# One VectorE instruction for both one-hot matrices of four tokens, with the weights multiplied in on ScalarE

## What is computed

```
q = (x @ w_q).reshape(T, PEER_HEADS, 2, PEER_DQH)
scores = einsum('thsd,hskd->thsk', q, sub_keys)        # 128 keys in each of two halves
s, i = top_k(scores, 16)
cand = s[:, :, 0, :, None] + s[:, :, 1, None, :]       # 16 x 16 pairs
top, sel = top_k(cand, 16)
idx = i0 * 128 + i1 of the selected pairs              # 8 heads x 16 experts a token
g = softmax(top)
a = gelu(einsum('td,thkd->thk', x, u_tab[idx]))
out = einsum('thk,thkd->td', g * a, v_tab[idx])
```

## Time and profile before

| | |
|---|---|
| median of 3 runs | 4314.09 us (4311.28 to 4319.12) |
| the profiled execution | 4313.75 us, span 4311.9 us |
| mean granted TensorE clock | 0.965 |
| busy: TensorE, VectorE, ScalarE, GpSimd | 94%, 61%, 11%, 33% of the span |
| layer 0, first scatter to last | 1228.9 to 1619.2 us |
| layer 1, first scatter to last | 3264.5 to 3622.3 us |

### The profile page before, as it was taken

One profiled execution on the slowest core, in us unless ns is written; L12 is line 12 of the kernel. 1 busy time (PEld: TensorE's weight loads), 2 busy tenths in 40 slices (PEclk: granted clock), 3 DMA queues, 4 the chain that ended last, 5 costly groups with the idle time before them and its releaser, 6 DMA issues.

```text
span 4311.9 us, 35262 instructions
## 1 busy us (share of the span) xinstructions
PE 4059.6 (94%) x12920; PEld 2247.2 (52%) x12920; DVE 2616.0 (61%) x5488; ACT 473.0 (11%) x879; POOL 1440.1 (33%) x1072
## 2 busy tenths in 40 slices
PE   8997899989999998999998999999999986999998
PEld 1655555555555663444444545666656664444443
DVE  2303577767767884433434954888887887443444
ACT  2010111101111220000001121111112221000000
POOL 0000014444445553333320000454555565333331
PEclk9998999999999998999999999999999986999999
DMA  8111247778889999888873100788889999888875
GB/s 318 60 58 62 93 171 288 282 269 314 313 314 348 355 343 374 318 331 322 316 281 123 59 30 20 280 313 298 328 330 342 353 330 321 356 328 321 321 304 184
DMA packets 349757, 1128.44 MB, mean 262 GB/s; under 512 B 23424, under 2 KB 139632, under 8 KB 328712
## 3 DMA queue, kind: packets, MB, share of 16 engines
q0 software_dynamic: 153632, 560.15, 35.2%
q1 hardware_dynamic: 96880, 515.69, 31.0%
q10 hardware_dynamic: 99072, 50.33, 3.9%
HBM read 1025.01 MB, written 101.07 MB: 261 GB/s over the span
## 4 chain that ended last, share of the span: by engine, by line
PE 88%; DMA 6%; DVE 5%; ACT 1%; issue 0%; SPq 0%; ACTq 0%; POOL 0%; DVEq 0%
PE bank L652 88%; DMA ring<-in_peer_ut 2%; DMA peer_gates<-work 2%; DMA ring<-in_peer_w_q 1%; DVE bc L1366 1%; DVE diag L1354 1%; DVE ring L1336 1%; DVE bc L1368 1%; DMA ring<-in_ada_w 1%; ACT work L952 0%; ACT hT L952 0%; DMA bc<-peer_gates 0%; DVE work L1190 0%; DVE work L1192 0%; PE bank L696 0%
## 5 line engine op out<-in xcount | busy, mean ns | idle before, releaser
L652 PE MATMUL bank<-hT,ring 128*128 128x384 f32 (+3 forms) x5696 | 1808.5, 477 | 59.5 <-DMA ring<-in_peer_ut 30.3
L652 PEld LDWEIGHTS bank<-hT,ring 128*128 128x128 f32 x5696 | 1062.0, 193 | 728.0 <-issue 89.2
L612 POOL DMA_INDIRECT ring<-in_peer_u,work x512 | 769.9, 1504 | 1728.4 <-DVE ring L1336 1456.6
L652 PE MATMUL bank<-ring,work 128*128 128x512 f32 x2016 | 868.8, 592 | 0.0
L612 POOL DMA_INDIRECT ring<-in_peer_v,work x512 | 644.5, 1259 | 302.1 <-issue 155.6
L1354 DVE SCALAR_TENSOR_TENSOR diag<-ring,work,diag 128x1024 f32<-128x1024 f32 x508 | 652.8, 1285 | 29.5 <-DMA ring<-in_peer_v,work 26.1
L1336 DVE SCALAR_TENSOR_TENSOR ring<-ring,work 128x1024 f32<-128x1024 f32 x512 | 622.2, 1215 | 22.7 <-DMA ring<-in_peer_u,work 22.7
L652 PEld LDWEIGHTS bank<-ring,work 128*128 128x128 f32 x2016 | 383.0, 190 | 482.2 <-issue 482.2
L1393 DVE TENSOR_TENSOR work<-work,bc 128x1536 f32<-128x1536 f32 x64 | 112.4, 1758 | 717.2 <-PE bank L652 666.0
L952 ACT ACTIVATE work<-bank 128x384 f32<-128x384 f32 (+3 forms) x540 | 290.7, 541 | 2029.8 <-PE bank L652 1928.6
L652 PE MATMUL bank<-work 128*128 128x512 f32 x1056 | 461.3, 597 | 30.8 <-DVE work L1393 30.8
(11 more groups left out here) (156 smaller groups left out, 1595.1 us busy)
## 6 DMA issues: line engine op xcount, KB each, us to landing
ring<-in_peer_ut SPq DMA_DIRECT2D x64, 2048.0 KB
ring<-in_peer_vt SPq DMA_DIRECT2D x42, 2048.0 KB, 7.9
ring<-in_ada_w SPq DMA_DIRECT2D x24, 2048.0 KB, 14.4
peer_gates<-work ACTq DMA_DIRECT2D x48, 1024.0 KB
bc<-peer_gates SPq DMA_DIRECT2D x32, 1536.0 KB
peer_acts<-work SPq DMA_DIRECT2D x60, 768.0 KB
work<-peer_acts SPq DMA_DIRECT2D x60, 768.0 KB, 15.1
work<-in_peer_vt SPq DMA_DIRECT2D x22, 2048.0 KB, 7.9
```

The lines of the kernel that those rows point to most:

```text
L612: nc.gpsimd.indirect_dma_start(row, None, table, bass.IndirectOffsetOnAxis(ap=idx_all[:, i:i + 1], axis=0)).then_inc(s, 16)
L652: return nc.tensor.matmul(out, lhsT, rhs, start=start, stop=stop, **kw)
```

## The change

`hot` no longer multiplies by the weights. One tensor_tensor compares both index rows of four tokens with the row 0..127 and writes all eight matrices. A new step `scale` on ScalarE then multiplies the first matrix of each of the four tokens by its weights, in place, and raises `oh_scaled`, for which `scatter` now waits. The planner's cost of a hot encoding falls from 2.1 to 1.3, and the times at which it deems the next steps due move. The other lines let several semaphores run on through both layers instead of having one for each layer.

```diff
-            picks += [("hot", b, g, 0, 2.1) for b in range(DB) for g in range(OHS)]
+            picks += [("hot", b, g, 0, 1.3) for b in range(DB) for g in range(OHS)]
...
                 if kind == "hot":
-                    ready.append((clock + 1, "scatter", a, b))
+                    ready.append((clock, "scale", a, b))
+                    ready.append((clock + 3, "scatter", a, b))
                     if b == OHS - 1 and a + 1 < DB:
-                        ready.append((clock + 1.5, "turn", a + 1, 0))
+                        ready.append((clock + 3.5, "turn", a + 1, 0))
...
                 def scatter(b, g):
                     i = sc_at[l]["scatter", b, g]
                     n = b * OHS + g
-                    pe.wait_ge(oh_ready[l], n + 1)
+                    pe.wait_ge(oh_scaled, l * DB * OHS + n + 1)
...
+                def scale(b, g):
+                    n = b * OHS + g
+                    act.wait_ge(oh_ready, l * DB * OHS + n + 1)
+                    for o in range(OH):
+                        last = f(oh[:, n % 2, 0, o, :], oh[:, n % 2, 0, o, :], scale=ijg_t[:, 2, g * OH + o:g * OH + o + 1])
+                    last.then_inc(oh_scaled, 1)
...
                     t0 = g * OH
-                    for o in range(OH):
-                        v.tensor_scalar(oh[:, n % 2, 0, o, :], iota, ijg_t[:, 0, t0 + o:t0 + o + 1],
-                                        ijg_t[:, 2, t0 + o:t0 + o + 1], ALU.is_equal, ALU.mult)
-                    v.tensor_tensor(oh[:, n % 2, 1, :, :], ijg_t[:, 1, t0:t0 + OH].unsqueeze(2).to_broadcast([P, OH, NKEYS]),
-                                    iota.unsqueeze(1).to_broadcast([P, OH, NKEYS]), ALU.is_equal).then_inc(oh_ready[l], 1)
+                    v.tensor_tensor(oh[:, n % 2, :, :, :], ijg_t[:, 0:2, t0:t0 + OH].unsqueeze(3).to_broadcast([P, 2, OH, NKEYS]),
+                                    iota.unsqueeze(1).unsqueeze(1).to_broadcast([P, 2, OH, NKEYS]), ALU.is_equal)\
+                        .then_inc(oh_ready, 1)
```

More of the change, by code:

```diff
@@ L305, in program @@
         own = Count(sem("peer_steps"))
-        top_ready = per_stage("top_ready", LAYERS); exp_ready = per_stage("exp_ready", LAYERS)
-        idx_ready = per_stage("idx_ready", LAYERS)
-        ijg_ready = sem("ijg_ready"); oh_ready = per_stage("oh_ready", LAYERS)
+        top_ready = sem("top_ready"); exp_ready = sem("exp_ready")
+        idx_ready = sem("idx_ready")
+        ijg_ready = sem("ijg_ready"); oh_ready = sem("oh_ready"); oh_scaled = sem("oh_scaled")
         sc_done = per_stage("sc_done", LAYERS); sc_taken = per_stage("sc_taken", LAYERS)
@@ L311, in program @@
         u_free = per_stage("u_free", LAYERS); v_free = per_stage("v_free", LAYERS)
-        gelu_ready = per_stage("gelu_ready", LAYERS)
+        gelu_ready = sem("gelu_ready")
         a_out = per_stage("a_out", 2); g_out = per_stage("g_out", 2)
@@ L316, in program @@
         w_ready = per_stage("w_ready", LAYERS)
-        v_done = per_stage("v_done", LAYERS); d_sums = per_stage("d_sums", LAYERS)
+        v_done = per_stage("v_done", LAYERS); d_sums = sem("d_sums")
         peer_gate_in = sem("peer_gate_in"); peer_gated = sem("peer_gated")
@@ L344, in program @@
                         for i in range(2)], CIN[c], (glu_sums, 2 * c + 2),
-                       ((u_free[0], ROWS), (v_free[0], ROWS), (d_sums[0], DB), (d_sums[0], DB))[c]) for c in range(4)]
+                       ((u_free[0], ROWS), (v_free[0], ROWS), (d_sums, DB), (d_sums, DB))[c]) for c in range(4)]
         before_cin = cin_c[0]
@@ L622, in peer_rows @@
                         if i % (GB * TOPK) == 0:
-                            pool.wait_ge(idx_ready[l], i // (GB * TOPK) + 1)
+                            pool.wait_ge(idx_ready, l * PHEADS + i // (GB * TOPK) + 1)
                         if i >= RING:
@@ L789, in peer @@
                         if n == CHUNKS - 1:
-                            last.then_inc(d_sums[l], 1)
+                            last.then_inc(d_sums, 1)
                     if n < CHUNKS - 1:
@@ L1031, in take_picks @@
                     if b:
-                        act.wait_ge(oh_ready[l], b * OHS)
+                        act.wait_ge(oh_ready, l * DB * OHS + b * OHS)
                     f(ijg_t.rearrange("p w t -> p (w t)"), bank[:, 4 + i % 2, 0:3 * P]).then_inc(sc_taken[l], 1)
+                def scale(b, g):
[4 more added lines that the diff above has]
+                    last.then_inc(oh_scaled, 1)
                 def take_scatter(b, g):
@@ L1053, in peer @@
                     elif kind == "exp":
-                        act.wait_ge(top_ready[l], a + 1)
-                        f(top_e, top_e, ACT.Exp).then_inc(exp_ready[l], 1)
+                        act.wait_ge(top_ready, l * PHEADS + a + 1)
+                        f(top_e, top_e, ACT.Exp).then_inc(exp_ready, 1)
                     elif kind == "gelu":
                         act.wait_ge(u_free[l], (a + 1) * TOPK)
-                        f(act16[:, a % 2, :], dots[:, a % 2, :], ACT.Gelu_apprx_tanh).then_inc(gelu_ready[l], 1)
+                        f(act16[:, a % 2, :], dots[:, a % 2, :], ACT.Gelu_apprx_tanh).then_inc(gelu_ready, 1)
                     elif kind == "turn":
                         take_picks(a)
+                    elif kind == "scale":
+                        scale(a, i)
                     elif kind == "scatter":
@@ L1300, in batch @@
                         v.tensor_tensor(top_e, top_v, top_v[:, :, 0:1].to_broadcast([P, BLOCKS, TOPK]), ALU.subtract)\
-                            .then_inc(top_ready[l], 1)
+                            .then_inc(top_ready, 1)
                         own.mark(v.tensor_scalar(pair[:, :, 0, :], top_i, 4, None, ALU.logical_shift_right))
@@ L1317, in batch @@
                         v.tensor_scalar(idx_all[:, rows_at].rearrange("p (b k) -> p b k", b=GB), part_i[:, 0:GB, 0, :],
-                                        float(l * EXPERTS), None, ALU.add).then_inc(idx_ready[l], 1)
-                        v.wait_ge(exp_ready[l], h + 1)
+                                        float(l * EXPERTS), None, ALU.add).then_inc(idx_ready, 1)
+                        v.wait_ge(exp_ready, l * PHEADS + h + 1)
                         own.mark(v.tensor_reduce(top_s, top_e, AX.X, ALU.add))
@@ L1339, in weight @@
                 def weight(n):
-                    v.wait_ge(gelu_ready[l], n + 1)
+                    v.wait_ge(gelu_ready, l * GH + n + 1)
                     own.mark(v.tensor_tensor(wgt[:, n % 2, :], act16[:, n % 2, :], g_all[:, n * TOPK:(n + 1) * TOPK], ALU.mult))
@@ L1400, in close @@
                     else:
-                        v.wait_ge(d_sums[l], b - GB + 1)
+                        v.wait_ge(d_sums, l * DB + b - GB + 1)
                         src, dst = bank[:, 2 * (b - GB):2 * (b - GB) + 2, :].rearrange("p c d -> p (c d)"), gated_d[:, b - GB, :]
```

## The result

The changed kernel takes 4420.76 us (median of four runs, 4417.33 to 4423.01) against 4312.68 us for the kernel before beside it: a ratio of 1.025, 95% interval 1.0232 to 1.0268. It is slower by 108 us, where 48 were forecast; the forecast's range ended at 4420. The profiled execution has a span of 4419.0 us, 107.1 more than before.

A forecast was written before the change was run, and what follows sets the result against it. TensorE was taken to bound the kernel, with VectorE the bound only in layer 1's tail. Layer 0 +42, layer 1 -14 and late gates' stores +20 summed to +48 on 4313.75 us: 4362 us, range 4300 to 4420.

The forecast's parts named there:

- VectorE's encoding and ScalarE's four scales: Each hot encoding: 1.23 us on VectorE, about 0.4 us saved; four scales on ScalarE end 1.28 us after the first starts.
- The waits: TensorE's scatter stretches: waits for encodings and scales within runs of scatters, 69.7 us in layer 0, 52.9 in layer 1.
- run of ten: Layer 1's last ten scatters: a pair follows a pair by 4.25 us, so ten take about 20 us.
- late second scale: A run's second scale, ordered behind the eviction of the job ahead, starts its scatter at 2.0 instead of 0.9: 1.1 lost.
- two slots: The oh buffer's two slots: a run's third encoding can't begin before the first scatter has ended; third scatter loses 2.1 us.
- rival (a): Whole kernel: VectorE's relief reaches the end, waits are half as long and stores land in time, 4281 us; chance 14%.
- Its work is the same, but its order isn't.: TensorE: same work, but scatters start 9 jobs later and packed; the order decides, with layer 0 +42 and layer 1 -14.
- rival (c): Scatter stretches: gaps cost TensorE's clock, 3.0 us at each of 22 runs of four, +66, near 4428 us; chance 15%.
- the 3.33 of its row: Wait of 3.33 us at layer 0's second turn before the change; next scatter and job took 3.0 us more together.
- The gap ahead of the values: End of layer 0: the gates' store is covered, only load and weighing are left, 8.6 us instead of 16.6.
- the 28 forecast without the stores: Both layers' scatter work and gates' wait, without late gates' stores: layer 0 +42 us and layer 1 -14 us.
- The stores' 20 us: ScalarE's evictions waiting for gates' stores: 18 late by 2 to 3 us, half reaching TensorE, 20 us; bounds 0 to 88.

The follow-up runs named there:

- scales early enough: Changed kernel with four oh slots instead of two and the scatter due 9 instead of 3 behind its encoding: 4339.84 us, ratio 1.0071.
- one constant: The kernel before with EARLY = 9 in place of 11, spreading choosing and encodings over 144 dots in place of 176: 4250.41 us, ratio 0.9864.
- two later versions: Changed kernel with four oh slots, late scatters, three gates' staging buffers: 4285.99 us; old encoding with four slots, three staging buffers, EARLY 9: 4263.83 us.

## Why the prediction was wrong

The direction was right, and so was the mechanism of the waits. The sum was 60 us short, because it left out what the waits cost the work beside them, and the time fell just above the range. The steps in turn:

**VectorE's encoding and ScalarE's four scales** came as forecast, 1224 ns against 1.23 us, and 1.28 us for four (2.43 for eight in the rows above). The Trainium skill's "VectorE: DVE Perf Modes" (section "The perf-mode tier table") has fp32 tensor_tensor a tier below tensor_scalar; the 1.9 us that the prediction estimated from this alone did not come, since the row of the same shape decides.

**The waits** were sized well: 69.7 us in layer 0 forecast and 67.5 idle measured; in layer 1 52.9, and 11 in the run of ten (its 20 us less ten scatters of 0.9), 63.9, against 58.1. The third scatter of a run mostly waits 1.85 (forecast 2.1), a late second scale 0.85 (1.1), a turn in layer 0 3.84 and 3.92 (4.0). That the sums come so close is in part luck, as a few waits are longer for reasons that were not in them. The two longest, of 4.56 us in the run of six and of 6.87 us, stand behind a scale that ScalarE reaches late, since it takes 2.52 us to issue a store, or waits 5.79 us for one; for the second:

```profile
1488.04 0.60 ACT L953 ACTIVATE work<-bank 128x512 f32<-128x512 f32 x1 [5.79 <-DMA peer_gates<-work]
1488.54 1.26 ACT L953 ACTIVATE bc<-bc 128x128 f32<-128x128 f32 x4
...
1489.85 2.07 PE L653 MATMUL bank<-bc 128*128 128x128 f32 x8 [6.87 <-ACT bc L953]
```

But "two slots", named against rival (a) as what forces them, is not the reason in this order: four slots changed nothing. What binds is the eviction ahead of the scale in ScalarE's order. The forecast's own sum has this (encoded at 2.32, evicted at 2.58); its words did not.

**The step that failed is "Its work is the same, but its order isn't."** The work was counted at before's durations. Without waits, layer 0's stretch should hold 370.8 us less 22 jobs of 5.16, 257, and layer 1's 251.2 less 9 jobs and plus 32 scatters of 0.895, 233. They hold 290.2 and 268.5: 33 and 35 us more. The run with filled waits takes 42 of these 68 to the granted clock. The other 26 stay although the clock is up. They are what a wait costs at full clock: a single scatter behind one shows 1.16 us, where scatters in a row come every 0.895, and a pair 2.33 in place of 1.95, since the second's scale ends 1.2 us behind the first's (the forecast has 0.3 for this among its waits). A piece of layer 1 at a granted clock of 1.00 shows the size:

```profile
3402.70:3460.10 57.40, 48.53 (x232) 33.94 (x232) 41.18 (x45) 31.93 (x89) 27.93 (x18) 1.00 0.90 316
```

Its 17 scatters and 6 jobs would take 46.2 us at 0.895 and 5.16. They take 48.5, 2.3 us more over five waits. At that rate all 72 waits would cost 34 us (an estimate), enough for the 26. So rival (c) had the larger part of the missing term. That its 66 us match the 68 is luck: it put them all down to the clock, to which the runs give 42. It was given 15% because a wait of 0.92 us had cost the scatter behind it nothing and the forecast's waits of 2 us lie between that and the 3.33 of its row. Three stretches of 20 us of layer 0 show that such waits can lower the clock:

```profile
1306.70:1326.70 20.00, 13.58 (x61) 10.28 (x60) 14.11 (x15) 9.52 (x27) 9.05 (x6) 0.83 1.01 372
1326.70:1346.70 20.00, 16.45 (x80) 11.44 (x79) 13.99 (x16) 11.58 (x33) 9.26 (x6) 1.00 0.72 213
...
1606.70:1626.70 20.00, 16.65 (x77) 11.69 (x75) 14.02 (x17) 12.49 (x36) 9.05 (x6) 0.91 0.97 341
```

```profile
1309.56 2.33 PE L653 MATMUL bank<-bc 128*128 128x128 f32 x16 [1.85 <-ACT bc L953]
1316.45 3.78 PE L653 MATMUL bank<-bc 128*128 128x128 f32 x16 [4.56 <-ACT bc L953]
1320.03 6.52 PE L653 MATMUL bank<-hT,ring 128*128 128x384 f32 x16
...
1614.26 2.78 PE L653 MATMUL bank<-bc 128*128 128x128 f32 x16 [1.85 <-ACT bc L953]
1616.84 6.60 PE L653 MATMUL bank<-hT,ring 128*128 128x384 f32 x16
```

A wait of 1.85 and one of 4.56 us stand in the first stretch; the two scatters behind the second take 3.78 us in place of 1.95, and the job 6.52 in place of 5.33. In the stretch after it, with a wait of 1.85 and two of 0.85, the clock is 1.00. In the third stretch no wait is longer than 1.85, and behind one of these the pair takes 2.78 us and the job 6.60. So not each wait pays, but enough of them do: 0.90 over the whole 357.7 us. The Trainium skill's "TensorE: Matmul & The Clock Gate" (section "HAM oscillation — how this bites in real kernels") describes the like in a kernel whose short bursts of matmuls stand between waits of 3 to 5 us for a DMA: the clock falls again and again. The traces here agree, with 0.90 and 0.91, and show it for shorter waits too.

**The rest of the accounting**, to the end of layer 1's last scatter (+107.0 us). Layer 0's values begin 89.4 us later, at 1725.24 (forecast 42). The first scatter is 57.8 us later, where nine jobs of 5.16 make 46.4: 11 us stay, of which TensorE's waits for loads of u explain 6.5 (32.5 against 26.0 us up to there) and the first scatter's own wait for its scale 1.74. Layer 1's first scatter has the same wait of 1.74, most of the 2 us by which it comes late. The gap ahead of the values is 13.8 us, not 8.6:

```profile
1712.06 11.08 DMA bc<-peer_gates
...
1725.24 4.92 PE bank L653 x7
```

No store stands in that chain any more, as forecast, but the load takes 11.08 us in place of 6.51. From there to the end of layer 1's last scatter it is 17.6 us more (forecast 14 less). The misses: work +68, idle time -8, first scatters +14 (11 and 2), the gap +5; together +79, and the 28 forecast without the stores make 107.

**The stores' 20 us** came only in part: ScalarE waited 21.0 us for them in all, less than before, and what reached TensorE is mainly the 5 us and 2.7 us by which the two longest waits exceed 1.85. The DMA engines were less busy (0.83 and 0.86 in the stretches, before 0.96 and 0.97), though the scatters came closer; that this is why the stores landed in time is not shown. The runs without scales, or with scales early enough, show this cost at once (50 and 91 us of TensorE). So the term was right as a danger, and mostly covered by the larger one.

**Where the 108 us come from**, by the runs: the new order 28 (old encoding in it), the merged encoding 14 less, the scales 93. (The three are the steps from before over two runs to after, so they must add up to the whole, 107; it is no check.) VectorE's relief never reached the end: the planner spent it on packing the scatters, and their scales came late in ScalarE's order.

What stays open is the exact split of the 68 us between the clock and what a wait costs at full clock, as the two taken apart make more (42 and 34), and why layer 0's first scatter comes some 3 us later than its jobs, loads and scale explain; in the five runs with the new order it lies between 1277.8 and 1286.7, so some of it may be variation between executions.

## What to carry to other kernels

When work moves to an idle engine that also evicts for TensorE, look at what stands ahead of it in that engine's order, not at its load: here 192 scales of 1.3 us on an engine busy a tenth of the time cost 93 us. Price a wait of TensorE at its length plus what the work beside it loses (here 126 us of idle time brought 68 us of slower work), and look for the next limiter before counting a gain. And try the numbers that place work before the instructions: one constant took 60 us off the kernel before.

## What the runs showed of the hardware

In the changed kernel, with waits mostly of 0.85 to 2.41 us between bursts of 2 to 9 us, the granted clock was 0.73 to 0.93 in 26 of 34 stretches of 20 us, and 1.00 in others with the same waits. Dummy matmuls in the waits brought it back to 0.97, and the time down by 20 us, although they overran the waits. A compare of 128x1024 with both inputs broadcast costs as much as an add of that size without (1224 and 1225 ns). Issuing a 1 MB store from ScalarE took 0.37 us as a rule, but up to 8.57 and 11.34 us in two later versions, in stretches with a DMA share of 0.98 and 0.94, and ScalarE did nothing else meanwhile.
